# Gate projection cut into quarters, one group in every stick-breaking unit, and four smaller moves at stage boundaries, in a one-layer hybrid encoder

## The reference

```python
def finish_layer(x, oa, ob, ga, gb, lp):
    mix = (jax.nn.sigmoid(ga) * (oa @ lp['w_oa']) + jax.nn.sigmoid(gb) * (ob @ lp['w_ob'])) @ lp['w_out']
    h = layer_norm(ALPHA * x + mix, lp['ln1_g'], lp['ln1_b'])
    f = hier_moe(h.reshape(-1, h.shape[-1]), lp).reshape(h.shape)
    return layer_norm(ALPHA * h + f, lp['ln2_g'], lp['ln2_b'])

def stick_breaking_block(q, t_idx, k, v):                     # branch B, blocks of 128 queries
    z = jnp.einsum('bqhd,bshd->bhqs', q, k).astype(jnp.float32) * HEAD_DIM ** -0.5
    before = jnp.arange(k.shape[1])[None, :] < t_idx[:, None]
    log_keep = jnp.where(before, jax.nn.log_sigmoid(-z), 0.0)
    log_later = lax.cumsum(log_keep, axis=3, reverse=True) - log_keep
    w = jnp.where(before, jnp.exp(jax.nn.log_sigmoid(z) + log_later), 0.0)
    return jnp.einsum('bhqs,bshd->bqhd', w.astype(v.dtype), v)
```

## Time and profile before

| | |
|---|---|
| three runs | 1783.58, 1792.64, 1793.36 us; median 1792.64 |
| profiled execution | 1796.71 us; its span 1794.9 |
| PE busy | 1644.9 us (92% of the span) |
| DVE, ACT, POOL busy | 1100.7, 843.2, 353.7 us |
| mean granted clock of PE | 0.955 |
| chain that ended last | PE 57%, issue 7%, DVE 4%, POOL 4%, DMA 2%, ACT 2% |

### The profile page before, as it was taken

The page is one execution under the profiler, slowest core; times in us unless marked ns, Lnnn a source line. Parts: engine busy times, 40 slices in busy tenths (PEclk is TensorE's granted clock), DMA queues, the critical chain, the costliest instruction groups (busy, mean ns, idle before and its releaser), DMA issues.

```text
span 1794.9 us, 28102 instructions
## 1 busy us (share of the span) xinstructions
PE 1644.9 (92%) x9608; PEld 1388.5 (77%) x9609; DVE 1100.7 (61%) x1697; ACT 843.2 (47%) x1308; POOL 353.7 (20%) x412
## 2 busy tenths in 40 slices
PE   8999999999999999989995999999999999998930
PEld 8988888687787789988874778888878888877730
DVE  3466564554535354552577874568986666888855
ACT  3134444333333333111222764567875555886754
POOL 0000000000000000002432332222334222333337
PEclk9999999899999999999996999999999999999975
DMA  4110100411111112542224976769997587999962
GB/s 186 44 34 25 36 25 16 164 49 33 49 47 46 48 49 105 191 139 78 79 96 165 348 268 234 266 253 400 408 397 264 210 320 292 382 390 373 363 257 99
DMA packets 64329, 324.17 MB, mean 181 GB/s; under 512 B 7680, under 2 KB 14464, under 8 KB 37600
## 3 DMA queue, kind: packets, MB, share of 16 engines
q1 hardware_dynamic: 52592, 280.68, 41.4%
q0 software_dynamic: 11664, 42.47, 6.8%
HBM read 280.36 MB, written 42.76 MB: 180 GB/s over the span
## 4 chain that ended last, share of the span: by engine, by line
PE 57%; issue 7%; DVE 4%; POOL 4%; DMA 2%; ACT 2%; POOLq 1%; ACTq 0%; DVEq 0%
PE ps L1012 6%; PE ps L1014 6%; PE ps L1013 6%; PE ps L832 3%; PE ps L1028 3%; PE ps L1030 3%; PE ps L1029 3%; PE ps L834 3%; PE ps L833 3%; PE ps L765 2%; DMA xg<-h_rows,idx 2%; PE ps L970 2%; PE ps L871 2%; PE ps L870 2%; PE ps L872 2%
## 5 line engine op out<-in xcount | busy, mean ns | idle before, releaser
L1760 DVE TENSOR_TENSOR we_lo<-we_raw,we_hi 128x1024 fp32r<-128x1024 f32 x384 | 449.5, 1220 | 32.7 <-ACT we_hi L1268 28.4
L1268 ACT ACTIVATE we_hi<-we_raw 128x1024 fp32r<-128x1024 f32 x384 | 378.0, 1052 | 40.8 <-issue 39.3
L1012 PE MATMUL ps<-we_hi,xb_hi 128*128 128x512 f32 x640 | 257.1, 402 | 5.5 <-DVE we_lo L1760 3.3
L1014 PE MATMUL ps<-we_hi,xb_lo 128*128 128x512 f32 x640 | 251.1, 392 | 0.0
L1013 PE MATMUL ps<-we_lo,xb_hi 128*128 128x512 f32 x640 | 250.3, 391 | 0.0
L545 PE MATMUL ps<-xT_hi,win_hi 128*128 128x358 f32 (+1 forms) x432 | 145.3, 336 | 8.1 <-DVE win_lo L1369 8.1
L1012 PEld LDWEIGHTS ps<-we_hi,xb_hi 128*128 128x128 f32 x640 | 120.8, 189 | 37.1 <-DVE we_lo L1760 11.4
L546 PE MATMUL ps<-xT_lo,win_hi 128*128 128x358 f32 (+1 forms) x432 | 141.4, 327 | 0.0
L1014 PEld LDWEIGHTS ps<-we_hi,xb_lo 128*128 128x128 f32 x640 | 120.7, 189 | 26.3
L547 PE MATMUL ps<-xT_hi,win_lo 128*128 128x358 f32 (+1 forms) x432 | 141.0, 326 | 0.0
L1013 PEld LDWEIGHTS ps<-we_lo,xb_hi 128*128 128x128 f32 x640 | 121.0, 189 | 23.6
(11 more groups left out here) (340 smaller groups left out, 3376.1 us busy)
## 6 DMA issues: line engine op xcount, KB each, us to landing
we_raw<-w_moe SPq DMA_DIRECT2D x192, 1024.0 KB, 7.5
win_raw<-w_u SPq DMA_DIRECT2D x18, 512.0 KB, 3.5
gates<-sgt SPq DMA_DIRECT2D x48, 176.0 KB, 1.8
back<-gates SPq DMA_DIRECT2D x8, 1056.0 KB, 5.8
wgate_raw<-w_mix SPq DMA_DIRECT2D x16, 512.0 KB, 3.6
yg<-y_rows SPq DMA_DIRECT2D x8, 1024.0 KB, 9.9
xT_raw<-xT SPq DMA_DIRECT2D x8, 536.0 KB, 8.2
kvb<-U SPq DMA_DIRECT2D x1, 4224.0 KB, 15.4
```

The lines of the kernel that those rows point to most:

```text
L1012: pe.matmul(o, xb_hi[:, k, :], e_hi[half][:, c], start=k == 0, stop=False)
L1014: last = pe.matmul(o, xb_lo[:, k, :], e_hi[half][:, c], start=False, stop=k == KD - 1)
L1268: act.activation(e_hi[n][:, c], e_raw[n][:, c], ACT.Copy).then_inc(s("d_hi" if n == 2 else "e_hi"), 1)
L1760: dve.tensor_tensor(e_lo[n][:, c], e_raw[n][:, c], as_f32(e_hi[n][:, c]), ALU.subtract).then_inc(s("d_split" if n == 2 else "e_split"), 1)
```

## The change

1. In branch B a gate third is cut into quarters of 6 matmuls, `gate_quarter`, all four into the same bank. `PIECES_BY` gives each unit three quarters, ahead of the turn or behind the values, by its place in a cycle of four units. ACT reads a third out in three units of four, and loads the next chunk's weights once in four. Only chunk 0 is split ahead of the loop. The next pair's q and k are staged one unit earlier.
2. The first pair's q and k are staged in two parts, 256 columns first; the sigmoid table is loaded ahead of ACT's two waits.
3. The first tile of `mT` is split for the output projection while DVE still mixes, into buffers that lie elsewhere; DVE's tables come after the first norm.
4. For the last tile of 32 rows, ACT's normalise and POOL's gain and bias are left out: DVE does them in two operations. Two splits of expert weights and two batches of `weights` stand elsewhere on DVE, and the last logits on PE ahead of four token matmuls.
5. In the tail, DVE's second sum also writes the row sum; the small operations for 1/std but the power, and the mean's product with it, go to ACT; the last tile's normalise, gain and bias are two DVE operations.

The core of the diff:

```diff
+QUARTERS = 4
+EARLY = 2 * P
+CYCLE = 4
+PIECES_BY = {0: ((), (0, 1, 2)), 1: ((3,), (4, 5)), 2: ((6, 7), (8,)), 3: ((9,), (10, 11))}
+
+def gate_pieces(n, late):
+    return [3 * QUARTERS * (n // CYCLE) + k for k in PIECES_BY[n % CYCLE][late]]
...
-            def gate_third(f):
+            def gate_quarter(g):
+                f, part = divmod(g, QUARTERS)
                 c, j = divmod(f, 3)
...
-                if j == 0:
-                    pe.wait_ge(s("gate_split"), c + 1)
-                if f == 0:
-                    pe.wait_ge(s("b_vsmall_out"), 2)
-                elif gate_bank(f) == GATE_B:
-                    pe.wait_ge(s("gate_sig"), f)
-                for k in range(KD):
+                if part == 0:
+                    if j == 0:
+                        pe.wait_ge(s("gate_split"), c + 1)
+                    if f == 0:
+                        pe.wait_ge(s("b_vsmall_out"), 2)
+                    elif gate_bank(f) == GATE_B:
+                        pe.wait_ge(s("gate_sig"), f)
+                for k in range(KD // QUARTERS * part, KD // QUARTERS * (part + 1)):
...
+                for g in gate_pieces(n, 0):
+                    gate_quarter(g)
                 b_turn(n)
                 if n:
                     b_values(n - 1)
-                if n in GATE_OF:
-                    gate_third(GATE_OF[n])
+                for g in gate_pieces(n, 1):
+                    gate_quarter(g)
...
             for n in range(NUNIT):
                 weigh(n + 1)
-                if (n + 1) % UPP == UPP - 1 and n + 1 < NUNIT - 1:
-                    act.wait_ge(s("b_z"), n + 2)
-                    stage_kq((n + 1) // UPP + 1)
+                if n % UPP == UPP - 3 and n + 3 < NUNIT:
+                    act.wait_ge(s("b_z"), n + 3)
+                    stage_kq(n // UPP + 1)
+                c, j = divmod(n, CYCLE)
+                if j in (1, 2):
+                    gate_sigmoid(3 * c + j - 1)
                 drain_turn(n)
...
+                if j == 3:
+                    gate_sigmoid(3 * c + 2)
+                if j == 1 and c + 1 < NGATE:
+                    gate_round(c + 1)
...
+            act.wait_ge(s("m_out"), 3 * KD - 1)
+            ms_round(0)
             act.wait_ge(s("m_out"), 3 * KD + 1)
-            ms_round(0)
...
-            dve.wait_ge(s("rstd"), 2 * NTL)
-            rest_third(2, 0, range(2))
+            last_row, last_mv = hkeep[0:DEC, NT, :], mv[NT % 2][0:DEC]
...
+            link(dve.scalar_tensor_tensor(out=last_row, in0=last_row, scalar=last_mv[:, 3:4], in1=g1[0:DEC, :],
+                                          op0=ALU.add, op1=ALU.mult))
             take_logits(NTL - 1)
             route(2)
+            dve.wait_ge(s("h_done"), NT)
+            dve.scalar_tensor_tensor(out=last_row, in0=last_row, scalar=last_mv[:, 4:5], in1=b1[0:DEC, :], op0=ALU.mult,
+                                     op1=ALU.add).then_inc(s("h_done"), 1)
...
             hidden(0, 0, True)
+            weights(1)
+            weights(2)
             rest_h(0, 0)
...
+                if t >= 2:
+                    dve.wait_ge(s("y_mean"), t - 1)
                 dve.scalar_tensor_tensor(out=f, in0=y[0:M, 1, :], scalar=prow[0:M, t, 1:2], in1=f, op0=ALU.mult,
-                                         op1=ALU.add).then_inc(s("y_sum"), 1)
+                                         op1=ALU.add, accum_out=mv[t % 2][0:M, 0:1]).then_inc(s("y_sum"), 1)
...
             def rstd2(t):
                 v = mv[t % 2][0:rows_of(t)]
-                pool.wait_ge(s("y_var"), t + 1)
-                pool.tensor_scalar(v[:, 3:4], v[:, 2:3], 1.0 / D, EPS / ALPHA ** 2, ALU.mult, ALU.add
-                                   ).then_inc(s("y_eps"), 1)
                 pool.wait_ge(s("y_eps"), t + 1)
```

More of the change, by code:

```diff
@@ L119 @@
 OUT_B, GATE_B = 6, 7
[L122 to L128, removed]
+QUARTERS = 4
+EARLY = 2 * P
+CYCLE = 4
+PIECES_BY = {0: ((), (0, 1, 2)), 1: ((3,), (4, 5)), 2: ((6, 7), (8,)), 3: ((9,), (10, 11))}
+assert NUNIT // CYCLE * 3 == NTHIRD - LATE and NUNIT % CYCLE == 0
+def gate_pieces(n, late):
+    return [3 * QUARTERS * (n // CYCLE) + k for k in PIECES_BY[n % CYCLE][late]]
 def gate_bank(f):
@@ L287, in build @@
         moe_small = r.at
-        ms_hi = [r.take(f"ms_hi{n}", [P, KD, P], F32R) for n in range(2)]
-        ms_lo = [r.take(f"ms_lo{n}", [P, KD, P], F32R) for n in range(2)]
+        b1 = r.take("b1", [P, D])
+        at_slot = [r.take(f"at_slot{n}", [P, P]) for n in range(RING)]
+        posx = r.take("posx", [P, TB, 2, NE])
+        assert r.at <= moe_small + 2 * 4096
+        ms_hi, ms_lo = ([None, r.take(f"ms_{n}1", [P, KD, P], F32R)] for n in ("hi", "lo"))
         xn = [r.take(f"xn{n}", [P, D]) for n in range(2)]
@@ L299, in build @@
         r = Region(after_m)
-        b1 = r.take("b1", [P, D])
+        ms_hi[0], ms_lo[0] = (r.take(f"ms_{n}0", [P, KD, P], F32R) for n in ("hi", "lo"))
         g2 = r.take("g2", [P, D])
@@ L328, in build @@
         colx = r.take("colx", [P, NTL, 2])
-        slot_at = r.at
-        at_slot = [r.take(f"at_slot{n}", [P, P]) for n in range(RING)]
+        rank_i = r.take("rank_i", [P, NCOL], I32)
         cnt_i = r.take("cnt_i", [P, NE], I32)
@@ L856, in _ @@
             s_values()
-            for f in range(NTHIRD - LATE, NTHIRD):
-                gate_third(f)
+            for g in range(QUARTERS * (NTHIRD - LATE), QUARTERS * NTHIRD):
+                gate_quarter(g)
             def mix_third(i, j):
@@ L1342, in moments, with settle_rows @@
                                ).then_inc(s("y_var"), 1)
+                act.wait_ge(s("y_var"), t + 1)
+                act.activation(v[0:M, 3:4], v[0:M, 2:3], ACT.Copy, scale=1.0 / D, bias=EPS / ALPHA ** 2
+                               ).then_inc(s("y_eps"), 1)
+            def settle_rows(t):
+                M, v, f = rows_of(t), mv[t % 2], yg[t % YB]
+                act.wait_ge(s("rstd"), 2 * NTL + t + 1)
+                act.activation(v[0:M, 5:6], v[0:M, 1:2], ACT.Copy, scale=v[0:M, 4:5]).then_inc(s("y_less"), 1)
+                act.wait_ge(s("y_less"), t + 1)
+                act.activation(f[0:M, 0, :], f[0:M, 0, :], ACT.Identity, bias=v[0:M, 5:6], scale=v[0:M, 4:5]
+                               ).then_inc(s("normed"), 1)
             moments(0)
@@ L1347, in _ @@
                     moments(t + 1)
[L1348 removed]
+                if t + 1 < NTL:
+                    settle_rows(t)
         @block.vector
@@ L1779, in _ @@
                     gain_routes()
+                    tables()
                 if t:
@@ L1948, in _ @@
                 rstd(t, M)
-                gain(t, h, g1[0:M, :])
-                pool.wait_ge(s("gained"), t + 1)
-                pool.tensor_tensor(h, h, b1[0:M, :], ALU.add).then_inc(s("h_done"), 1)
+                if t < NTL - 1:
+                    gain(t, h, g1[0:M, :])
+                    pool.wait_ge(s("gained"), t + 1)
+                    pool.tensor_tensor(h, h, b1[0:M, :], ALU.add).then_inc(s("h_done"), 1)
             pool.wait_ge(s("rows_out"), 16 * NTL)
```

157 lines of the change are left out of this document (86 added, 71 removed).

## The result

The changed kernel takes 1741.13 us (median of 4 runs, 1735.57 to 1745.06), before 1793.0 (4 runs, 1783.58 to 1797.32): ratio 0.9715, 95% interval 0.9668 to 0.9763, so 52 us faster by the medians. The prediction said 1756 with a range of 1739 to 1775: the direction and the range hold, the gain was put at 37 and is 52.

A forecast was written before the change was run, and what follows sets the result against it. PE, busy in 92% of the span, bounds the kernel; gains come from its idle time, half clock and the tail. -6 - 15 - 7 - 5 - 2 - 2 = -37 takes the median 1792.6 to 1756 us, range 1739 to 1775.

The forecast's parts named there:

- A: The forecast itself for the whole kernel: 1756 us, by itself 1747 to 1765; chance 0.50.
- rival B: Whole kernel: groups cost only 0.05 each and the tail loses part of its 6.1 a tile, 1742 to 1748; chance 0.20.
- Start and rest of the stage: Stick-breaking stage: -6 at its start, -15 in the rest as PE's waits and half clock go, less group costs.
- I take 0.16 a group, 9.8 in all: Stick-breaking stage: switching cost of 60 extra gate groups, 0.16 us each; bounds 3 and 15 in all.
- the three later pairs: Stick-breaking stage: staging q and k earlier removes PE's wait for ql at the three later pairs' starts.
- Rival D: Gate thirds sharing one PSUM bank wait for ACT's read-out, 1.2 us a third: slower by 17, 1810; chance 0.04.
- Start: Start of the stick-breaking stage: earlier first scores and gate quarters from unit 0 end the half clock, -6; bounds -9, -2.
- Mix to output projection: Between mix and output projection: first tile split while PE mixes, -4.7 of waiting and -2.3 of half clock, -7.
- Plan: Last tile's plan: PE's 11.60 wait for seen shrinks as DVE and POOL stop holding each other up, -5; bounds -3, -7.
- First expert block: Small weight operations on DVE move earlier, shortening PE's 3.25 wait for we_lo, -2; bounds 0, -2.2.
- Tail: After PE's last matmul: still 6.1 a tile, shorter way into the first gain and shorter last tile, -2; bounds -10, +2.
- The exclusion: Tail: DVE and POOL don't run large operations at once, so a tile stays 6.1; without it about 4.8.

The follow-up runs named there:

- old tail: Changed kernel with the tail of the kernel before: 1749.80 us, ratio 0.9781 to the kernel before.
- first pair at full width: Changed kernel with the first pair's q and k staged at full width and the table load behind the waits, as before: 1750.84 us, ratio 0.9777.
- one group a unit: Changed kernel with the three gate quarters of every unit in one group behind the values, 60 groups in place of 105: 1761.90 us, ratio 0.9852.
- tail on DVE: Changed kernel with every tail tile's norm as two DVE operations, no normalise on ACT and no gain on POOL: 1738.45 us, ratio 0.9729.
- late third: Changed kernel with the first of the three late gate thirds ahead of the decode unit's values: 1742.65 us, ratio 0.9713.
- both: Changed kernel with a late gate third ahead of the decode unit's values and every tail tile's norm on DVE: 1738.54 us, ratio 0.9701.
- without the stage: Kernel before with parts 3 to 5 of the change, everything but the stick-breaking stage: 1765.80 us, ratio 0.9872.
- the stage alone: Kernel before with only parts 1 and 2 of the change, the stick-breaking stage: 1761.58 us, ratio 0.9847.

## Why the prediction was right and where it wasn't

*The total.* 1741 lies in the range, but below the forecast's own band (A, 1747 to 1765) and 1 us below rival B's (1742 to 1748). Both halves of B came true, as said below: cheap groups, and a tail that loses a part of its 6.1. A part of the gain is luck in the expert stage. Six kernels below with that same expert stage (old tail, first pair at full width, one group a unit, tail on DVE, late third, both) differ from the changed kernel in the other pieces by amounts that the profiles give. Less these, their medians put the change at 37 to 51 us, 44 in the mean (an estimate).

*Start and rest of the stage, -21 forecast, -28.0.* The mechanism was right: with gate work in every unit, the waits for wgt and ql go (idle 21.1 to 3.7, with the wait ahead of the first matmul) and most of the half clock with them. For these the forecast had 30.9 (6 at the start, 15.7 less 1 of waits, 10.2 of clock), and 32.4 came. The term that was mis-sized is the cost of the cuts, "I take 0.16 a group, 9.8 in all": it is some 4.4, 0.07 a group, near the lower bound of 0.05, which was rival B's. I had priced an entry and an exit of a group and not asked which steps they replace. The kernel with 150 groups shows that it isn't a price for each group at all: its 45 more cost nothing where they stand. The wait for ql at "the three later pairs" stood at one of them only (3.1).

*Rival D* didn't come true, and its price was too high: the bank's wait costs 0.72 where it is open (30 places), not 1.2, and in the changed kernel no wait for the read-out is left.

*Start.* Up to 336 us PE's idle time goes from 3.7 to 1.8, and its busy time at half clock from 16.3 to 3.2: 8.4 won, -6 forecast, before the groups' cost. Of the two causes that the prediction names the gate quarters count; the narrow first staging is worth 0.7.

*Mix to output projection, -7 forecast, -4.8 and -1.4.* As worked out; the half clock that went gave 1.4 of its 2.3.

*Plan, -5 forecast, -3.6; up to -5.6 in others.* From PE's last L970 (now L981) to the place matmuls it is 17.20 before (938.96 to 956.16) and 11.99 now (905.47 to 917.46): 5.2. In the changed kernel's profile 1.6 go again further on. This goes with the clock: it is 0.62 over the piece here, which takes 32.28, and 0.69 to 0.70 in the kernels without the stage, with the old tail and with the tail on DVE, which take 30.25 to 30.35. Why the half clock lasts longer in some executions was not tried.

*First expert block, -2 forecast, -2.0* (the wait for we_lo). The other 11.6 of the expert stage in the two profiles are 6.3 of waits for gathered rows and a clock that is at half for 15.7 us of the stage before and 3.1 now. This is luck, as far as the profiles tell: with the code of before the stage took 746.49 and 736.30, with the changed code from 732.67 to 744.51. Without the 11.6 the two profiled executions would lie some 45 apart, and the medians (52, with an interval of 42 to 60) allow that.

*Tail, -2 forecast, -6.2.* The exclusion was right: 3.36 for a sum beside POOL's gain, and a tail that shrinks to 61.4 when POOL's work goes to DVE. But "the same four operations still add up to 6.1" is wrong: a tile takes 5.87. The hand-overs between the two engines have become shorter. The gain, which stood waiting, ends 2.2 behind DVE's L1936 (1693.85 to 1696.04), where the gain in the earlier trace rows takes 2.35; the held sum ends 1.1 behind the gain, where it takes 1.28 by itself. From the first to the eighth L1936 this and a shorter last step (3.46, 4.48 before) bring 2.6 (41.22 before, 38.61 now). The way into the first shift is 12.09 before and 10.80 now (1.3, forecast 1.2). The last tile is the larger miss: from its neighbour's shift to the end 9.22 before and 6.87 now, 2.35 where I took 1.0, mainly because that shift was held for 2.0 by the last tile's gain (4.48 for two of 1.23), in front of the last store.

## What to carry to other kernels

Price a piece of work that is put between two others by all the steps from start to start that it makes, the first one inside it too, less those that it replaces. A cut between long groups of matmuls can be free or nearly so, and then its place is decided by what it covers: a bank's read-out, a scan, a conversion. Where a bank or a buffer is shared, keep other work between its last use and the next. Moving work from POOL to a busy DVE can shorten a stage when the two exclude each other, and the profile shows it as one long instruction beside the other's.

## What the runs showed that I had not expected

A late gate third removed from its place (1.5 us won) uncovered a split that it had hidden (2.3 us of waiting, 4.2 lost in all): work that seems to be filling at the end of a stage can be the cover of the next. The half clock in the decode unit's values doesn't need a wait ahead of it: with none it came at 663.0 for 10.2 us, and in the kernel with both changes for 3.4 us only (666.3 to 669.7). And one expert stage, unchanged, took from 736 to 746 us in the profiles of the kernel before and of the stage alone.
